# High and low activation parts side by side in the first expert weights of a two-block network, with GpSimd making every other low part of the weights

## The reference, cut to what matters

```python
q = (xc @ w_q).reshape(PEER_CHUNK, PEER_HEADS, 2, half)
sc = jnp.einsum('thpd,hpnd->thpn', q, subkeys).astype(jnp.float32)
s1, i1 = lax.top_k(sc[:, :, 0], PEER_TOPK)
s2, i2 = lax.top_k(sc[:, :, 1], PEER_TOPK)
...
```

## Time and profile before

| | |
|---|---|
| median of 3 runs | 2436.85 us (2436.35 to 2437.56) |
| the profiled execution, its own time | 2436.76 us |
| its span in the trace | 2435.0 us |
| mean granted TensorE clock | 0.991 |
| PE busy | 2363.0 us, 97% |
| DVE / ACT / POOL busy | 1706.1 / 1261.8 / 139.0 us |
| stage of first expert weights, layer 0 | about 257 to 700 us of the span |
| the same, layer 1 | up to about 1675 us |

### The profile page before, as it was taken

The page is one execution under the profiler, slowest core; times in us unless marked ns, Lnnn a source line. Parts: engine busy times, 40 slices in busy tenths (PEclk is TensorE's granted clock), DMA queues, the critical chain, the costliest instruction groups (busy, mean ns, idle before and its releaser), DMA issues.

```text
span 2435.0 us, 37993 instructions
## 1 busy us (share of the span) xinstructions
PE 2363.0 (97%) x14940; PEld 2120.8 (87%) x14940; DVE 1706.1 (70%) x3118; ACT 1261.8 (52%) x2070; POOL 139.0 (6%) x167
## 2 busy tenths in 40 slices
PE   8999999999999999999999999999999999987999
PEld 7778999999988888776799999998888788766997
DVE  6566599888865555667759988886555666755775
ACT  3454544566645544545444456665545554655444
POOL 0000000022200000000000002220000000000000
PEclk9999999999999999999999999999999999988999
DMA  7455556544466666743455664446667575332565
GB/s 239 149 180 174 163 176 190 182 131 131 131 189 192 202 196 191 215 148 104 150 163 179 187 181 133 130 136 183 193 195 219 175 216 171 104 96 70 182 184 162
DMA packets 111536, 407.40 MB, mean 167 GB/s; under 512 B 12528, under 2 KB 12576, under 8 KB 111104
## 3 DMA queue, kind: packets, MB, share of 16 engines
q1 hardware_dynamic: 107568, 391.36, 53.4%
q0 software_dynamic: 3072, 12.04, 1.5%
q10 hardware_dynamic: 720, 1.57, 0.2%
HBM read 403.87 MB, written 1.05 MB: 166 GB/s over the span
## 4 chain that ended last, share of the span: by engine, by line
PE 86%; DVE 5%; ACT 4%; DMA 3%; issue 1%; POOLq 0%; ACTq 0%; DVEq 0%
PE ps L560 13%; PE ps L563 13%; PE ps L557 13%; PE ps L624 9%; PE ps L628 9%; PE ps L620 9%; PE ps L789 5%; PE ps L591 3%; PE ps L588 3%; PE ps L595 3%; DMA raw<-in_peer_v 3%; PE ps L665 1%; DVE lo L1745 1%; ACT hi L1217 1%; PE ps L763 1%
## 5 line engine op out<-in xcount | busy, mean ns | idle before, releaser
L1745 DVE TENSOR_TENSOR lo<-raw,hi 128x1024 fp32r<-128x1024 f32 x678 | 830.5, 1227 | 510.3 <-ACT hi L1217 508.6
L1217 ACT ACTIVATE hi<-raw 128x1024 fp32r<-128x1024 f32 x678 | 715.6, 1057 | 633.8 <-PE ps L628 283.8
L557 PE MATMUL ps<-xh,hi 128*128 128x256 f32 x2720 | 391.3, 287 | 12.1 <-ACT hi L1217 12.1
L560 PE MATMUL ps<-xl,hi 128*128 128x256 f32 x2720 | 382.6, 283 | 0.0
L563 PE MATMUL ps<-xh,lo 128*128 128x256 f32 x2720 | 382.1, 283 | 0.0
L557 PEld LDWEIGHTS ps<-xh,hi 128*128 128x128 f32 x2720 | 350.1, 192 | 12.7 <-ACT hi L1217 12.1
L560 PEld LDWEIGHTS ps<-xl,hi 128*128 128x128 f32 x2720 | 351.7, 192 | 0.0
L563 PEld LDWEIGHTS ps<-xh,lo 128*128 128x128 f32 x2720 | 351.3, 192 | 0.0
L620 PE MATMUL ps<-hi,lh 128*128 128x512 f32 x988 | 305.6, 390 | 8.9 <-ACT lh L1254 8.9
L624 PE MATMUL ps<-hi,ll 128*128 128x512 f32 x988 | 305.6, 391 | 2.3 <-DVE ll L1810 2.3
L628 PE MATMUL ps<-lo,lh 128*128 128x512 f32 x988 | 305.1, 390 | 0.0
(11 more groups left out here) (353 smaller groups left out, 2417.8 us busy)
## 6 DMA issues: line engine op xcount, KB each, us to landing
raw<-in_peer_u SPq DMA_DIRECT2D x256, 512.0 KB, 3.6
raw<-in_peer_v SPq DMA_DIRECT2D x256, 512.0 KB, 4.1
raw<-in_ret_vg SPq DMA_DIRECT2D x32, 512.0 KB, 4.1
raw<-in_peer_q SPq DMA_DIRECT2D x24, 512.0 KB, 3.6
raw<-in_ffn_up SPq DMA_DIRECT2D x22, 512.0 KB, 4.2
raw<-in_ffn_down SPq DMA_DIRECT2D x22, 512.0 KB, 3.6
raw<-in_ffn_gate SPq DMA_DIRECT2D x18, 512.0 KB, 4.0
raw<-in_ret_qk SPq DMA_DIRECT2D x16, 512.0 KB, 5.4
```

Of the source, the lines that this page charges most:

```text
L557: e.matmul(out, uh[:, k, :], xh[:, k, :], start=k == 0, stop=False)
L560: e.matmul(out, uh[:, k, :], xl[:, k, :], start=False, stop=False)
L1217: e.activation(parts(i)[0][:, 0:w], raw[:, i % N_RAW, 0:w], ACT.Copy).then_inc(s_hi, 1)
L1745: e.tensor_tensor(ul[:, 0:w], raw[:, i % N_RAW, 0:w], uh[:, 0:w].bitcast(F32), ALU.subtract).then_inc(s_lo, 1)
```

## The change

PE: the units of `peer_u` are multiplied by `feat_wide` in place of `feat`. High and low part of the activations now lie side by side in one tile `xs` (8, 2, 256), so that `hi` meets both as 512 moving columns in eight matmuls that fill a whole bank: columns 0 to 255 collect hi.xh, columns 256 to 511 hi.xl. The eight matmuls of `lo` with `xh` add to the first half. A pair now takes two banks of the ring of four, and waits for both.

ACT copies the second halves of a pair to SBUF (`half`), DVE adds them to the first halves in PSUM (`add`), ACT applies gelu (`gelu`), DVE multiplies (`gated`). There is one room for the copied halves, which lies over a place of the rings `lh` and `ll`. The four steps of pair c-1 stand among the work of pair c: ACT's `half` before the `hi` of its first unit and `gelu` behind it, DVE's `add` at its first unit and `gated` at its second. Those of pair 63 stand in the first steps of `peer_v`.

POOL makes `lo` of the odd units of `peer_u` (`low_part`), counted by a semaphore `s_lop` of its own; whoever needs `lo` of unit n (PE, SP's queue) asks `low(n)` which semaphore to wait for. Its builds of one-hot rows now stand at the same places as those of the other engines.

```diff
+    def claim_pair(self, key, ring, filled, freed=None):
+
+        b = self.at[ring] % 4 + ring
+        assert b % 2 == 0
+        self.at[ring] += 2
...
+        xs = sb("xs", [128, 8, 2, S], F32R)
+        xh, xl = xs[:, :, 0, :], xs[:, :, 1, :]
...
+        by_pool = {W.first[f"peer_u{l}"] + i: 64 * l + i // 2 + 1 for l in range(2) for i in range(1, 128, 2)}
...
+            def halves_of(l):
+
+
+                return halves_room[:, :, L.ring[lhs_first[f"peer_v{l}"] + 2], :]
...
+                e.wait_ge(s_hi, n + 1)
+                for k in range(8):
+                    xs_there(0, gen, 1, k)
+                    xs_there(1, gen, 1, k)
+                    e.matmul(out, uh[:, k, :], xs[:, k, :, :].rearrange("p h t -> p (h t)"), start=k == 0, stop=False)
+                e.wait_ge(*low(n))
+                for k in range(8):
+                    ins = e.matmul(out[:, 0:S], ul[:, k, :], xh[:, k, :], start=False, stop=k == 7)
+                ins.then_inc(s_used, 1)
...
-                    u = claim(("u", l, c), UPPER, filled=(s_used, n + 2),
-                              freed=None if TOKENS[c] else (s_gelu, 64 * l + c + 1))
+                    u = psum.claim_pair(("u", l, c), UPPER, (s_used, n + 2), None if TOKENS[c] else (s_gelu, 64 * l + c + 1))
+                    for before in u.before:
+                        e.wait_ge(*before)
...
+                def half(c):
+
+                    u = use["u", l, c]
+                    if c:
+                        e.wait_ge(s_added, 64 * l + c)
+                    e.wait_ge(*u.filled)
+                    e.activation(halves_of(l), u.view[:, :, S:2 * S], ACT.Copy).then_inc(s_half, 1)
+
+                def gelu(c):
+                    u, t0 = use["u", l, c], TOKENS[c]
+                    e.wait_ge(s_added, 64 * l + c + 1)
...
                 for c in range(64):
-                    u, t0 = use["u", l, c], TOKENS[c]
                     for j in range(2):
+                        if c and j == 0:
+                            half(c - 1)
                         feat_units(f"peer_u{l}", 2 * c + j, 1)
+                        if c and j == 0:
+                            gelu(c - 1)
...
+                def add(c):
+
+                    sums = use["u", l, c].view[:, :, 0:S]
+                    e.wait_ge(s_half, 64 * l + c + 1)
+                    e.tensor_tensor(sums, sums, halves_of(l), ALU.add).then_inc(s_added, 1)
...
+                    for j in range(2):
+                        if c:
+                            (gated if j else add)(c - 1)
                         units(f"peer_u{l}", 2 * c + j, 1)
...
+            def low_part(n):
+                uh, ul = parts(n)
+                e.wait_ge(s_hi, n + 1)
+                e.tensor_tensor(ul, raw[:, n % N_RAW, :], uh.bitcast(F32), ALU.subtract).then_inc(s_lop, 1)
...
+            def beside_experts(l):
+
+                n0 = W.first[f"peer_u{l}"]
+                low_part(n0 + 1)
+                for c in range(64):
+                    for j in range(2):
+                        if j == 1 and c < 63:
+                            low_part(n0 + 2 * c + 3)
+                        for i in STEPS_AT[c, j]:
+                            if i < 64:
+                                build(l, i)
...
                 if n >= N_RAW:
-                    e.wait_ge(s_lo, n - N_RAW + 1)
+                    e.wait_ge(*low(n - N_RAW))
```

More of the change, by code:

```diff
@@ L51, in claim @@
         return self.claim_bank(key, b, filled, freed)
+    def claim_pair(self, key, ring, filled, freed=None):
+        b = self.at[ring] % 4 + ring
+        assert b % 2 == 0
+        self.at[ring] += 2
+        u1 = self.claim_bank((key, 1), b + 1, filled, freed)
+        u0 = self.claim_bank((key, 0), b, filled, u1.freed)
+        u = self.use[key] = Use(self.ps[:, b:b + 2, :], (u0.before, u1.before), filled, u1.freed)
+        return u
     def claim_bank(self, key, b, filled=None, freed=None):
@@ L340, in xs_count, with low @@
             return 4 * gen + (k // 2 if gen == X_RET else 2 * t + k // 4) + 1
+        by_pool = {W.first[f"peer_u{l}"] + i: 64 * l + i // 2 + 1 for l in range(2) for i in range(1, 128, 2)}
+        lows = [0]
+        for n in range(len(W.src)):
+            lows.append(lows[-1] + (n not in by_pool))
+        def low(n):
+            return (s_lop, by_pool[n]) if n in by_pool else (s_lo, lows[n + 1])
         def landed(n):
@@ L1401, in ready, with last @@
                     return [use["u", l, 63].freed] if k == EARLY_EXPERTS else []
-                acc(f"peer_v{l}", 128, lambda k: experts[:, k, :], ready, after=after, early=6, more=more)
+                def last(k):
+                    if k == 0:
+                        half(63)
+                        gelu(63)
+                acc(f"peer_v{l}", 128, lambda k: experts[:, k, :], ready, before=last, after=after, early=6, more=more)
             peer(0, more=4)
@@ L1741, in lo_to @@
                 for i in range(at["lo"], n + 1):
[L1742 to L1746, removed]
+                    if i not in by_pool:
+                        e.wait_ge(s_hi, i + 1)
+                        w = W.src[i].shape[-1]
+                        uh, ul = parts(i)
+                        e.tensor_tensor(ul[:, 0:w], raw[:, i % N_RAW, 0:w], uh[:, 0:w].bitcast(F32),
+                                        ALU.subtract).then_inc(s_lo, 1)
                 at["lo"] = max(at["lo"], n + 1)
@@ L2086, in peer, with last @@
                                             ALU.mult).then_inc(s_selT, 1)
-                acc(f"peer_v{l}", 128, lambda k: experts[:, k, :], after=after, early=6, more=more)
+                def last(k):
+                    if k == 0:
+                        add(63)
+                    if k == 1:
+                        gated(63)
+                acc(f"peer_v{l}", 128, lambda k: experts[:, k, :], before=last, after=after, early=6, more=more)
             peer(0, 0, "ret_w_out", more=4)
@@ L2632, in pool, with build @@
             ln_load(0, 0)
[L2634 to L2642, removed]
+            def low_part(n):
+                uh, ul = parts(n)
+                e.wait_ge(s_hi, n + 1)
+                e.tensor_tensor(ul, raw[:, n % N_RAW, :], uh.bitcast(F32), ALU.subtract).then_inc(s_lop, 1)
+            def build(l, i):
+                if i == 0:
+                    e.wait_ge(s_const, 64)
+                    e.wait_ge(s_norm, 8 * l + 4)
+                    e.wait_ge(s_selT, 2 * l + 2)
+                if i >= 2:
+                    e.wait_ge(*use["G", l, i - 2].filled)
+                e.tensor_scalar(Peer.oha[i % 2][:, 0, :], iota[:, :], selT[:, 1, 4 * i:4 * i + 1],
+                                selT[:, 2, 4 * i:4 * i + 1], ALU.is_equal, ALU.mult).then_inc(s_ohp, 1)
+            def beside_experts(l):
[8 more added lines that the diff above has]
+                                build(l, i)
                 e.wait_ge(*use["u", l, 63].freed)
```

47 lines of the change are left out of this document (26 added, 21 removed).

## The result

The changed kernel takes 2451.57 us (2446.93 to 2452.58, 5 runs) against 2436.85 of the kernel before: a ratio of 1.0054, 95% interval 1.0039 to 1.0068. It is slower by 0.5% where 1.0% faster was forecast. Its profiled execution has a span of 2449.8 us, 14.8 more than before.

A forecast was written before the change was run, and what follows sets the result against it. PE, busy 97% of the span, was taken to bound the kernel. Wide matmuls -27.3, turned gates +5.0 and end of the stage -2.2 sum to -24.5 us, from 2436.76 to 2412.3; range 2406 to 2438.

The forecast's parts named there:

- PE bounds the kernel, and a wide matmul saves time: Units of `peer_u`: PE sets the time; eight wide matmuls save 0.107 us a unit, -27.3 us in all.
- POOL, low part: On POOL, one low part a pair takes 2.37 us of the pair's 5.55 us.
- POOL's queue: One-hot build behind the low part: ready after 4.3 us, needed a unit later, over 7 us; no cost.
- DVE beside POOL: Placing gates: each low part takes 0.8 to 1.6 us from DVE, 14.2 to 15.8 against 15.54; PE loses nothing.
- rival B: Placing gates: POOL and DVE exclude each other for POOL's whole instruction, up to +47 us, 2442 to 2459; chance 0.13.
- The ring of pairs: Two banks a pair are freed in time: 3.3 us to spare early, 5.0 of 7.3 us at placing.
- The turned gates: Between pairs 34 and 35, PE waits 2.5 us a layer until pair 34 is freed: +5.0 us.
- The end of the stage: After pair 63, PE's 1.1 us wait for the first `lh` goes, twice: -2.2 us.
- A: Placing gates: partial gain, DVE near its limit, PE sometimes waits for the product freeing a pair; 2419 to 2432; chance 0.15.
- C: Units of `peer_u`: the wide matmul doesn't bring what it should; 2432 to 2440; chance 0.12.

The follow-up runs named there:

- e3: The changed kernel with 256-column matmuls again, one bank a pair, no copy or add, POOL's low parts kept; 2453.32 us, ratio 1.0059.
- e8: e3 with POOL's first one-hot build of each unit ahead of the low part; 2437.26 us, ratio 0.9997.
- e1: The changed kernel with every low part made by DVE again, none by POOL; 2441.46 us, ratio 1.0011.
- e2: The changed kernel with POOL making odd low parts of pairs 0 to 32 alone, DVE all others; 2433.83 us, ratio 0.9983.
- e7: e2 with the turned gates in the idle LOWER ring in place of UPPER; 2421.46 us, ratio 0.9934.
- e4: The changed kernel with DVE's add of pair 34 ahead of its copies of the turned gates; 2441.93 us, ratio 1.0012.

## Why the prediction was wrong

The sum was -24.5 us in a range of 2406 to 2438; the time is 2451.57. In the sum's own terms:

- **PE bounds the kernel, and a wide matmul saves time** ("-27.3 us"): right in kind, -20.7 measured. The pace of the other stage was 226.7 ns, here it is 230. Why 3 ns more, no run here shows. By the Trainium skill, "TensorE: Matmul & The Clock Gate", section "Back-to-back issue gap", as the prediction worked it out, it would have been 5.1 us; the trace disagrees.
- **POOL, low part**: "I take 2.37": 2.40 in the median. The duration was right.
- **POOL's queue** ("It is needed by PE a unit later", "Nothing"): the step that failed first. It holds for the first step of a unit and not for the second of a two-step unit, whose build is needed in the same unit. 1.06 + 2.4 + 0.9 = 4.4 us against a unit of 3.7. I had counted the steps in `STEPS_AT` and not asked what PE spreads in which of them. e3 against e8 shows the price: 7.8 us of placing in layer 0. With the next point, which stands on the same units, it cost 15.0 us over both layers in the changed kernel, where the sum had nothing.
- **DVE beside POOL** ("0.8 to 1.6 us from DVE", "I take no loss for PE"): the second failure, and rival B's mechanism was the right one. I scaled a `lo` that was 0.10 us longer beside a POOL instruction of 128 elements, as if the engines shared a width. They take turns, and what was held was not so much `lo` as the one-hot tensor-scalars: up to 2.2 us each. The row of the 0.10 us was no guide, for a build holds DVE far less than a low part does. Rival B put its price at up to 2459, for DVE losing 2.37 us to each low part; it loses about that where it is held, but PE loses only what reaches the two-step units. That 2451.6 lies within B's 2442 to 2459 is partly luck, for its sum is not what happened. The argument against B, that POOL can't hold anything for all of 2.37 us, is false by the row at 598.09. The argument for it, a POOL build of 1.75 us, was on the table and got too little weight. It is the first of the two in this row of the trace before, and it ended 0.77 us behind the `lo` that DVE had begun ahead of it:

```profile
1452.34 1.23 DVE L1745 TENSOR_TENSOR lo<-raw,hi 128x1024 fp32r<-128x1024 f32 x1
1452.59 2.76 POOL L2641 TENSOR_SCALAR lnp<-iota,selT 128x128 f32<-128x128 f32 x2 [275.57 <-DVE negT L2085]
```

- **The ring of pairs**: right while gates are placed; PE never waited there for DVE's product. Beside the top-k I gave 3.3 us to spare and the waits are 3.6 us a layer. DVE's add comes late behind long top-k products. Each of the three waits follows one of the three pairs of bf16 products that took 5.63 or 5.64 us with a low part between them instead of 3.54, and these 2.1 us are more than any of the waits. So the exclusion is the likely cause here too, but this is argued from DVE's queue; no run has the ring of pairs beside the top-k with neither low parts on POOL nor a full DVE (e1, without low parts on POOL, waits 5.0 us there since DVE is full).
- **The turned gates** ("+5.0 us"): place, order and releaser right, 4.2 and 4.45 us instead of 2.5, and 1.7 us a layer for the clock, which the sum didn't have. The held tensor-scalar is 1.7 us of the wait in layer 0 and 1.9 in layer 1, the whole difference from 2.5. e2, where it takes 0.19 us again, still waits 3.93, for there DVE makes one low part more, 1.14 us ahead of the copies. e7 shows the ring as the cause of the wait.
- **The end of the stage** ("-2.2 us"): right.
- **Rivals A and C**: A had the place and the size (7 to 20 us, 15.0 measured), but it named DVE's product, for which PE never waited while gates were placed. C is false: three quarters of the gain came.

## What to carry to other kernels

Before work moves to POOL, list what DVE does at the same time by its operands. In these traces whatever read twice from SBUF, and the one-hot tensor-scalars, waited until POOL's 2.4 us low part was through; what had an operand in PSUM did not, nor did maxima and index searches. Low parts ahead of 64 one-hot builds in POOL's queue cost the narrow kernel 7.8 us a layer (e3), and behind the first build of each unit nothing (e8). And for each instruction behind a moved one, ask in which step its result is needed at the earliest, not as a rule; a schedule that now and then does two steps in a unit has its deadline there.

## What the runs showed of the hardware

- DVE's instructions with two SBUF inputs or of the tensor-scalar kind and POOL's low part exclude each other, both ways: a 0.34 us tensor-scalar took up to 2.53 us, a 2.40 us low part up to 4.06. Beside POOL's 0.8 us builds the same tensor-scalar took at most 0.45.
- A matmul has a cost beside its columns: two of 256 columns 240.0 ns, one of 512 columns 226.7 to 230 at a granted clock of 1.00.
- After PE had stood for 4.2 us at the turned gates, the granted clock was 0.51 for the next 3.5 us; after the waits of 1.66 us beside the top-k the eight wide matmuls are listed with 2.09 us, near the 2.00 of full clock. A wait of 3.4 us (e1) had eight wide ones of 3.55 us behind it. The wait of 2.06 us in layer 0 of e4 cost 1.6 us of clock, spread over the next 24 matmuls; the one of 1.86 us in its layer 1 cost none.
- The time of a stretch that no edit was meant to touch differed by up to 5 us between the profiled executions. For costs under 5 us the stretch in the timeline decided here, not the total.
